# Stick-breaking attention: both heads of a narrow key block in one step, and the rounding on VectorE

## The chip, the cores and the metric

The kernel runs on one core of a Trainium2 chip. Its time is device time in microseconds (us) of one launch. The engines of the core work side by side, each through its own list of instructions in order, and wait for each other by semaphores: TensorE (PE in the rows; matrix products, results go to PSUM, eight banks of 512 fp32 columns), VectorE (DVE), ScalarE (ACT), GpSimd (POOL) and SyncE (SP, which here issues the loads).

## The reference

The kernel computes two transformer blocks over 512 tokens of width 1024. The change touches the attention of the very last layer, "stick-breaking" attention with 12 heads of 64:

```
z = einsum("bhtd,bhsd->bhts", qb, kb) * scale
causal = s_idx < t_idx
log_not = where(causal, log_sigmoid(-z), 0.0)
tail = cumsum(log_not, axis=3, reverse=True) - log_not
log_a = log_sigmoid(z) + tail
a = where(causal, exp(log_a), 0.0)
out = einsum("bhts,bhsd->bhtd", a, vb)
```

A query t gives key s the weight exp(z - sum of softplus(z) over the keys from s up to t), so each key's weight needs the sum over all later keys. All is computed to fp32 accuracy.

## The kernel before

The program is one long pipeline: feed-forward parts and projections (most of the time, TensorE's split products of lines 947 to 949), attention parts between. Weights come as units of 128 x 1024; ScalarE rounds a unit to its high part and GpSimd subtracts to get the low part. Each engine's order is written out by hand in its own function.

In the stick-breaking stage keys lie on the partitions and queries in the columns. A chunk c is a pair of heads (2c, 2c+1), which lie in the two 64-row halves of a tile; there are 6 chunks. A chunk takes its four key blocks of 128 from the last, j = 3, to the first, j = 0. Key block j is seen by 512 - 128 j queries, so the widths are 128, 256, 384, 512. A step is one head and one block (48 steps), a round is the two steps of a block (24 rounds). Step t uses PSUM bank t % 6, so three rounds are in flight. Its way is:

- TensorE `sb_scores` (L1362): z of the step.
- VectorE `sb_clip_` (L1807): min(z, 40) into a slot. ScalarE `sb_exp_ln` (L905, L907): ln(1 + exp). VectorE `sb_soft` (L1817): the maximum of that and z, which is softplus; then L1818 multiplies the 128 columns of the diagonal block by the causal mask.
- ScalarE `sb_round` (L915): the high part XH. GpSimd `low_softplus` (L481): the low part XL. Eight slots of each are kept, since the sums of a block need the later blocks of the same head.
- TensorE `sb_tail` (L1374): subtracts the sums, a product for the high and one for the low part of each block at or behind j, 2 to 8 a step, into the scores' bank. Then L1376 adds a large negative number above the diagonal.
- ScalarE `sb_weights` (L922): exp, the weights. TensorE `sb_values` (L1387): their product with v into bank 6 or 7. VectorE `sb_take` (L1800): the chunk's result out of PSUM.

What sets the order: TensorE's loop over rounds does scores of round i, tail sums of i-2 (`LAG_T` 4 steps), values of i-3 (`LAG_V` 6 steps), and scores wait until the weights of round i-3 have been taken from their bank. ScalarE does for each t: weights of step t-4, exp and ln of t, rounding of t-1. VectorE: clip of t, then maximum and mask of t-1.

Of the kernel before, what the change touches and what calls it, by code (L numbers as in the profile page):

```python
# [230 lines left out]
LAG_T = 4  # L231
LAG_V = 6
SBANKS = 6


def program(nc, xT, memT, wstream, small, consts, constsb, out):
# [4 lines left out]
    with ctx:  # L241
# [38 lines left out]
        RSTDM = sb("RSTDM", [P, M])  # L280
        PS = ctx.enter_context(nc.psum_tensor("PS", [P, 8, S], F))
# [7 lines left out]
        ASLOT = [PB[:, 2, :], PB[:, 3, :], W[:, 20, :], W[:, 21, :]]  # L289
        ESLOT = [PT[:, 0, :], PT[:, 1, :], TMP[:, 0, :], TMP[:, 1, :]]  # L290
# [83 lines left out]
        sb_l, sb_hi, sb_lo = sem("sb_l"), sem("sb_hi"), sem("sb_lo")  # L374
        sb_tri, sb_a, sb_pv, sb_o = sem("sb_tri"), sem("sb_a"), sem("sb_pv"), sem("sb_o")
# [3 lines left out]
        SBSTEPS = [(2 * c + r, j) for c in range(6) for j in range(NT - 1, -1, -1) for r in range(2)]  # L379
# [61 lines left out]
        def _(pool):  # L441
# [34 lines left out]
            def low_softplus():  # L476

                for t, (h, j) in enumerate(SBSTEPS):
                    w = S - j * P
                    pool.wait_ge(sb_hi, t + 1)  # L480
                    pool.tensor_tensor(XL[:, t % 8, 0:w], PB[:, t % 2, 0:w], XH[:, t % 8, 0:w].bitcast(F),  # L481
                                       ALU.subtract).then_inc(sb_lo, 1)
# [19 lines left out]
        def _(act):  # L502
# [398 lines left out]
            def sb_exp_ln(t):  # L901

                e = ESLOT[t % 4][:, 0:S - SBSTEPS[t][1] * P]
# [5 lines left out]
            def sb_round(t):  # L909

                w = S - SBSTEPS[t][1] * P
                act.wait_ge(sb_l, t + 1)
                if t >= 8:
                    act.wait_ge(sb_tri, t - 1)
                act.activation(XH[:, t % 8, 0:w], PB[:, t % 2, 0:w], ACT.Copy).then_inc(sb_hi, 1)  # L915

            def sb_weights(t):
                w = S - SBSTEPS[t][1] * P
# [3 lines left out]
                act.activation(ASLOT[t % 4][:, 0:w], PS[:, t % SBANKS, 0:w], ACT.Exp).then_inc(sb_a, 1)  # L922
# [21 lines left out]
        def _(pe):  # L944
# [409 lines left out]

            n = len(SBSTEPS)

            def sb_scores(t):
                h, j = SBSTEPS[t]
                if t >= SBANKS:
                    pe.wait_ge(sb_a, (t | 1) - SBANKS + 1)  # L1360
# [603 lines left out]
```

## Time and profile before

| what | us |
|---|---|
| median of three runs | 2361.65 |
| the runs | 2356.34 to 2362.01 |
| the profiled execution | 2363.2 |
| its span | 2361.4 |

TensorE is busy for 2258.7 us of the span, GpSimd 975.1, VectorE 976.8, ScalarE 841.4. The page cuts the span into 40 slices of 59 us; the stage described lies in slices 32 and 33, where TensorE's busy digits are 7 and 8, and the load engines stand nearly still (19 and 1 GB/s). "Busy" of TensorE overlaps between products that run one behind the other, so the starts of its instructions say more than their durations.

### The profile page before, as it was taken

The page shows a single profiled execution, that of the slowest core. Times are in us where ns is not written, and L with a number is a line of the kernel's source. Part 1 is how long each engine was busy: PE and PEld are TensorE (multiplying, and loading weights), DVE is VectorE, ACT ScalarE, POOL GpSimd, SP SyncE. Part 2 cuts the span into 40 slices and gives each one's busy share as a digit, 9 for nine tenths or more (in the row PEclk, how much of TensorE's full clock was granted, in tenths as well). Part 3 has the DMA queues.
Part 4 walks back from the last instruction along what each step waited for, and adds up shares of the span by engine and source line. Part 5 has one row for each costly group of instructions (what it writes and reads, how often), then busy time and mean ns, then how long its engine had stood idle before and what let it go on. Part 6 is the DMA issues. An engine that isn't in the chain of part 4 may idle for free.

```text
span 2361.4 us, 28298 instructions
## 1 busy us (share of the span) xinstructions
PE 2258.7 (96%) x10366; PEld 1781.8 (75%) x10366; DVE 976.8 (41%) x1433; ACT 841.4 (36%) x1410; POOL 975.1 (41%) x435
## 2 busy tenths in 40 slices
PE   8999999998889899999999999999999789999997
PEld 6888887874446688888777888888877458888886
DVE  3112347356674511134675421124552663211344
ACT  4222235323663422223443332222342763322222
POOL 4444444551002544444453354444443433544442
PEclk9999999998889999999999999999999989999999
DMA  5222332331001132223232232222222002322222
GB/s 184 89 106 89 107 107 89 125 125 36 1 1 38 70 107 89 107 89 118 78 107 72 90 107 91 104 89 107 80 95 76 19 1 72 122 92 93 103 89 71
DMA packets 29801, 202.67 MB, mean 86 GB/s; under 512 B 3360, under 2 KB 4000, under 8 KB 6048
## 3 DMA queue, kind: packets, MB, share of 16 engines
q1 hardware_dynamic: 28800, 198.55, 23.9%
q10 hardware_dynamic: 928, 3.14, 0.4%
q8 instruction: 46, 0.75, 0.1%
q14 instruction: 27, 0.22, 0.0%
HBM read 198.54 MB, written 2.10 MB: 85 GB/s over the span
## 4 chain that ended last, share of the span: by engine, by line
PE 87%; DVE 5%; ACT 4%; issue 2%; POOL 1%; ACTq 0%; DVEq 0%; POOLq 0%
PE PS L947 26%; PE PS L949 26%; PE PS L948 26%; PE PS L1270 1%; PE PS L1239 1%; DVE ACC L1430 1%; PE PS L1374 1%; PE PS L1198 1%; PE PS L1362 1%; DVE TMP L1510 1%; DVE NMAX L1662 1%; POOL X L471 1%; PE PS L1018 1%; PE PS L1094 0%; DVE PB L1681 0%
## 5 line engine op out<-in xcount | busy, mean ns | idle before, releaser
L446 POOL TENSOR_TENSOR WL<-RAW,WH 128x1024 fp32r<-128x1024 f32 x368 | 908.8, 2473 | 1276.0 <-ACT WH L512 1276.0
L947 PE MATMUL PS<-XH,WH 128*128 128x512 f32 (+1 forms) x2200 | 866.9, 394 | 30.4 <-DVE XL L1422 20.9
L949 PE MATMUL PS<-XH,WL 128*128 128x512 f32 (+1 forms) x2200 | 853.4, 388 | 0.0
L948 PE MATMUL PS<-XL,WH 128*128 128x512 f32 (+1 forms) x2200 | 853.1, 388 | 0.0
L512 ACT ACTIVATE WH<-RAW 128x1024 fp32r<-128x1024 f32 x368 | 388.1, 1059 | 1262.2 <-PE PS L949 1218.3
L947 PEld LDWEIGHTS PS<-XH,WH 128*128 128x128 f32 x2200 | 415.3, 189 | 126.6 <-issue 27.5
L948 PEld LDWEIGHTS PS<-XL,WH 128*128 128x128 f32 x2200 | 415.7, 189 | 85.8 <-issue 4.1
L949 PEld LDWEIGHTS PS<-XH,WL 128*128 128x128 f32 x2200 | 415.1, 189 | 84.8
L949 PE MATMUL PS<-HH,WL 128*128 128x512 f32 x672 | 261.7, 389 | 0.0
L948 PE MATMUL PS<-HL,WH 128*128 128x512 f32 x672 | 261.7, 389 | 0.0
L947 PE MATMUL PS<-HH,WH 128*128 128x512 f32 x672 | 261.7, 389 | 0.0
L1453 DVE TENSOR_TENSOR Y<-RSTD,PS 128x512 f32<-128x512 f32 x88 | 60.5, 687 | 379.9 <-PE PS L949 379.9
L1477 DVE TENSOR_TENSOR HL<-WORK,HH 128x512 fp32r<-128x512 f32 x60 | 140.8, 2346 | 185.1 <-ACT HH L671 172.8
L1451 DVE TENSOR_TENSOR TMP<-RSTD,PS 128x512 f32<-128x512 f32 x88 | 60.5, 688 | 306.0 <-PE PS L949 294.9
L949 PEld LDWEIGHTS PS<-HH,WL 128*128 128x128 f32 x672 | 126.2, 188 | 26.2
L948 PEld LDWEIGHTS PS<-HL,WH 128*128 128x128 f32 x672 | 126.2, 188 | 26.1
L947 PEld LDWEIGHTS PS<-HH,WH 128*128 128x128 f32 x672 | 126.2, 188 | 26.1
L1422 DVE SCALAR_TENSOR_TENSOR XL<-X,SM,XH 128x512 fp32r<-128x512 f32 x64 | 66.0, 1048 | 67.4 <-ACT XH L525 67.4
L1430 DVE TENSOR_TENSOR ACC<-ACC,SQ 128x512 f32<-128x512 f32 x66 | 57.2, 866 | 34.5 <-ACT SQ L534 30.3
L1456 DVE TENSOR_TENSOR WORK<-SQ,Y 128x512 f32 (+1 forms) x88 | 63.7, 723 | 18.5 <-ACT SQ L646 7.5
L1662 DVE TENSOR_REDUCE NMAX<-PS 128x1 f32<-128x256 f32 (+4 forms) x160 | 59.0, 410 | 22.9 <-PE PS L1210 12.7
L481 POOL TENSOR_TENSOR XL<-PB,XH 128x128 fp32r<-128x128 f32 (+3 forms) x48 | 41.8, 871 | 61.4 <-ACT XH L915 61.4
(194 smaller groups left out, 1639.3 us busy)
## 6 DMA issues: line engine op xcount, KB each, us to landing
RAW<-wstream SPq DMA_DIRECT2D x183, 1024.0 KB, 4.8
X<-xT SPq DMA_DIRECT2D x4, 512.0 KB, 9.4
WORK<-memT ACTq DMA_DIRECT2D x2, 1024.0 KB, 5.5
outT<-WORK SPq DMA_DIRECT2D x8, 256.0 KB, 2.1
RAW<-wstream SPq DMA_DIRECT2D x2, 512.0 KB, 6.5
PB<-WORK ACTq DMA_DIRECT2D x8, 127.8 KB, 2.4
CST<-consts SPq DMA_DIRECT2D x1, 912.0 KB, 12.1
WORK<-constsb SPq DMA_DIRECT2D x1, 256.0 KB, 12.7
```

The source lines that it names most:

```text
L446: pool.tensor_tensor(WL[:, s, :, :].rearrange("p a b -> p (a b)"), RAW[:, s, :], WH[:, s, :, :].rearrange("p a b -> p (a b)").bitcast(F), ...
L512: act.activation(WH[:, v % RING, :, :].rearrange("p a b -> p (a b)"), RAW[:, v % RING, :], ACT.Copy).then_inc(hi_done, 1)
L947: pe.matmul(o, wh, xh, start=start, stop=False)
L948: pe.matmul(o, wh, xl, start=False, stop=False)
L949: return pe.matmul(o, wl, xh, start=False, stop=stop)
L1422: dve.scalar_tensor_tensor(lo, src, gain(name, k), hi.bitcast(F), ALU.mult, ALU.subtract).then_inc(xn_ready, 1)
L1430: dve.tensor_tensor(ACC[:, :], SQ[:, 0, :] if k == 1 else ACC[:, :], SQ[:, k % 2, :], ALU.add).then_inc(sq_added, 1)
L1451: dve.tensor_tensor(TMP[:, s, :], RSTD[:, :], PS[:, 2 * s, :], ALU.mult).then_inc(g_scaled, 1)
L1453: dve.tensor_tensor(Y0[:, :], RSTD[:, :], PS[:, 2 * s + 1, :], ALU.mult).then_inc(gu_free, 1)
L1456: dve.tensor_tensor(h, SQ[:, s, :], Y0[:, :], ALU.mult).then_inc(h_ready, 1)
L1477: dve.tensor_tensor(HL[:, s, :], W[:, bass.ds(i * 2 + (s + 2), 1), :].rearrange("p a b -> p (a b)"), HH[:, s, :].bitcast(F), ALU.subtract) ...
L1662: dve.tensor_reduce(NMAX[:, s:s + 1], PS[:, score_bank(y, j), 0:y["n"]], AX.X, ALU.max, negate=True).then_inc(nmax_ready, 1)
```

## The change

Steps change. Where both heads' queries fit in a bank together (2 x width <= 512, so j = 3 and j = 2) one step holds both heads, in neighbouring columns of one bank; the blocks j = 1 and j = 0 keep a step and a bank for each head. A chunk has then six steps of widths 256, 512, 384, 384, 512, 512 and still four rounds (lists `SBSTEPS` and `SBROUNDS`). Each round has its own banks (0, 1, 2+3, 4+5), so four rounds are in flight.

The mask moves: the large negative number is added right behind the scores, before the clip, and the multiply is gone. A masked softplus is then 0 by itself. In a paired step TensorE computes the first head, adds its mask, waits for its own first product (`sb_first`) and computes the second head.

The rounding moves from ScalarE to VectorE: `sb_round` takes the same maximum a second time, straight into XH. The fp32 softplus goes to four slots (two of them in the new tile LT).

```
@@ -228,9 +228,9 @@
-LAG_T = 4
-LAG_V = 6
-SBANKS = 6
+LAG_T = 3
+LAG_V = 4
+LAG_A = 3
...
+        LSLOT = [PB[:, 0, :], PB[:, 1, :], LT[:, 0, :], LT[:, 1, :]]
...
-        SBSTEPS = [(2 * c + r, j) for c in range(6) for j in range(NT - 1, -1, -1) for r in range(2)]
+        SBSTEPS, SBROUNDS = [], []
+        for _c in range(6):
+            for _j in range(NT - 1, -1, -1):
+                _own = [(0, 1)] if 2 * (S - _j * P) <= S else [(0,), (1,)]
+                SBROUNDS.append([len(SBSTEPS) + n for n in range(len(_own))])
+                SBSTEPS += [dict(c=_c, j=_j, heads=heads, w=S - _j * P) for heads in _own]
+        SBCHUNK = len(SBSTEPS) // 6
...
+        def sb_bank(t):
+            x = SBSTEPS[t]
+            return PS[:, NT - 1 - x["j"] if len(x["heads"]) == 2 else 4 - 2 * x["j"] + x["heads"][0], 0:sb_width(t)]
...
ScalarE
-            def sb_round(t):
-                w = S - SBSTEPS[t][1] * P
-                act.wait_ge(sb_l, t + 1)
-                if t >= 8:
-                    act.wait_ge(sb_tri, t - 1)
-                act.activation(XH[:, t % 8, 0:w], PB[:, t % 2, 0:w], ACT.Copy).then_inc(sb_hi, 1)
...
-            for t in range(n + LAG_T):
-                if t >= LAG_T:
-                    sb_weights(t - LAG_T)
+            for t in range(n + LAG_A):
                 if t < n:
                     sb_exp_ln(t)
-                if 1 <= t <= n:
-                    sb_round(t - 1)
+                if t >= LAG_A:
+                    sb_weights(t - LAG_A)
...
TensorE
+            def sb_scores(i):
+                if i >= NT:
+                    pe.wait_ge(sb_a, SBROUNDS[i - NT][-1] + 1)
+                parts = [(t, h) for t in SBROUNDS[i] for h in SBSTEPS[t]["heads"]]
+                if len(SBROUNDS[i]) == 1:
+                    (t, a), (_, b) = parts
+                    sb_products(t, a).then_inc(sb_first, 1)
+                    sb_strict(t, a)
+                    pe.wait_ge(sb_first, sum(len(r) == 1 for r in SBROUNDS[:i + 1]))
+                    sb_products(t, b)
+                    sb_strict(t, b).then_inc(sb_qk, 1)
+                else:
+                    for t, h in parts:
+                        sb_products(t, h)
+                    for t, h in parts:
+                        sb_strict(t, h).then_inc(sb_qk, 1)
...
+            for i in range(len(SBROUNDS) + LAG_V):
+                if i < len(SBROUNDS):
+                    sb_scores(i)
+                if 0 <= i - LAG_T < len(SBROUNDS):
+                    for t in SBROUNDS[i - LAG_T]:
+                        sb_tail(t)
+                if i >= LAG_V:
+                    sb_values(i - LAG_V)
...
VectorE
+                dve.tensor_tensor(LSLOT[t % 4][:, 0:w], ESLOT[t % 4][:, 0:w], sb_bank(t), ALU.max).then_inc(sb_l, 1)
+            def sb_round(t):
+                w = sb_width(t)
+                dve.wait_ge(sb_ln, t + 1)
+                if sb_slot_free(t):
+                    dve.wait_ge(sb_tri, sb_slot_free(t))
+                dve.tensor_tensor(XH[:, t % 8, 0:w], ESLOT[t % 4][:, 0:w], sb_bank(t), ALU.max).then_inc(sb_hi, 1)
+            for t in range(n + SBCHUNK + 1):
                 if t < n:
                     sb_clip_(t)
+                if 2 <= t <= n + 1:
+                    sb_round(t - 2)
                 if 1 <= t <= n:
                     sb_soft(t - 1)
```

`sb_slot_free(t)` is the number of tail sums after which the high part's slot of step t is free. In the new kernel's rows below L1378 is the score product, L1382 the mask addition, L1413 the tail sums, L1426 the values; on VectorE L1845 the clip, L1853 the maximum, L1861 the rounding maximum; on ScalarE L936 and L938 exp and ln, L944 the weights.

TensorE before, from the tail sums of a 256-wide round to the scores of the next chunk's 128-wide round (x2: both heads):

```order
L1374 MATMUL PS<-XH,SUMS 128x256
L1374 MATMUL PS<-XL,SUMS 128x256
L1374 MATMUL PS<-XH,SUMS 128x128
L1374 MATMUL PS<-XL,SUMS 128x128
L1376 MATMUL PS<-CSB 128x128
L1374 MATMUL PS<-XH,SUMS 128x256
L1374 MATMUL PS<-XL,SUMS 128x256
L1374 MATMUL PS<-XH,SUMS 128x128
L1374 MATMUL PS<-XL,SUMS 128x128
L1376 MATMUL PS<-CSB 128x128
L1387 MATMUL PS<-PB,WORK 64x128 x2
L1362 MATMUL PS<-WORK 128x128 x2
```

TensorE after, the same kind of place:

```order
L1426 MATMUL PS<-PB,WORK 64x512 x2
L1378 MATMUL PS<-WORK 128x128
L1382 MATMUL PS<-CSB 128x128
L1378 MATMUL PS<-WORK 128x128
L1382 MATMUL PS<-CSB 128x128
L1413 MATMUL PS<-XH,SUMS 128x256
L1413 MATMUL PS<-XL,SUMS 128x256
L1413 MATMUL PS<-XH,SUMS 128x128
L1413 MATMUL PS<-XL,SUMS 128x128
L1413 MATMUL PS<-XH,SUMS 128x256
L1413 MATMUL PS<-XL,SUMS 128x256
L1413 MATMUL PS<-XH,SUMS 128x128
```

The two narrow score products no longer stand next to each other; each has its mask addition behind it, and the mask additions are gone from the tail sums.

ScalarE before, from an exp of a 512-wide step (TMP and PT are the slots, PB and WORK take weights):

```order
L905 ACTIVATE TMP<-TMP 128x512
L907 ACTIVATE TMP<-TMP 128x512
L915 ACTIVATE XH<-PB 128x384
L922 ACTIVATE WORK<-PS 128x256
L905 ACTIVATE TMP<-TMP 128x512
L907 ACTIVATE TMP<-TMP 128x512
L915 ACTIVATE XH<-PB 128x512
L922 ACTIVATE PB<-PS 128x384
```

ScalarE after, from the weights of a 512-wide step:

```order
L944 ACTIVATE PB<-PS 128x512
L936 ACTIVATE PT<-PT 128x384
L938 ACTIVATE PT<-PT 128x384
L944 ACTIVATE PB<-PS 128x512
L936 ACTIVATE PT<-PT 128x384
L938 ACTIVATE PT<-PT 128x384
L944 ACTIVATE WORK<-PS 128x256
```

The rounding into XH has left the list, and between two weights there are only exp and ln.

VectorE before, around 128-wide and 256-wide steps:

```order
L1807 TENSOR_SCALAR PT<-PS 128x128
L1817 TENSOR_TENSOR PB<-PT,PS 128x128
L1818 TENSOR_TENSOR PB<-PB,CST 128x128
L1807 TENSOR_SCALAR TMP<-PS 128x256
L1817 TENSOR_TENSOR PB<-PT,PS 128x128
L1818 TENSOR_TENSOR PB<-PB,CST 128x128
L1807 TENSOR_SCALAR TMP<-PS 128x256
L1817 TENSOR_TENSOR PB<-TMP,PS 128x256
L1818 TENSOR_TENSOR PB<-PB,CST 128x128
```

VectorE after, around 384-wide and 512-wide steps:

```order
L1845 TENSOR_SCALAR PT<-PS 128x384
L1861 TENSOR_TENSOR XH<-TMP,PS 128x512
L1853 TENSOR_TENSOR PB<-PT,PS 128x384
L1845 TENSOR_SCALAR TMP<-PS 128x512
L1861 TENSOR_TENSOR XH<-PT,PS 128x384
L1853 TENSOR_TENSOR PB<-PT,PS 128x384
L1845 TENSOR_SCALAR TMP<-PS 128x512
L1861 TENSOR_TENSOR XH<-PT,PS 128x384
L1853 TENSOR_TENSOR LT<-TMP,PS 128x512
```

The short multiply (L1818) has gone; a second full-width maximum, into XH, stands before the next step's maximum.

## Rows read from the trace of the kernel before

**Rows 1.** The page's first line, and the busy shares under it.

```profile
span 2361.4 us, 28298 instructions
...
PE 2258.7 (96%) x10366; PEld 1781.8 (75%) x10366; DVE 976.8 (41%) x1433; ACT 841.4 (36%) x1410; POOL 975.1 (41%) x435
```

**Rows 2.** Windows, the stage: length, busy time by engine, clock, DMA share, GB/s.

```profile
1833.00:1942.00 109.00, 86.00 (x484) 56.06 (x484) 71.61 (x150) 78.59 (x198) 43.70 (x49) 0.89 0.01 2
```

**Rows 3.** Waits, 1833 to 1942: us in total, times, longest.

```profile
ACT XH L915 <- PE PS L1376: 21.6, 19, 2.3
...
PEld PS L1362 <- ACT PB L922: 17.0, 11, 1.7
...
PEld PS L1362 <- ACT WORK L922: 14.3, 10, 2.1
```

**Rows 4.** Timeline of TensorE, one chunk: start, duration, instruction, idle before it.

```profile
1867.47 0.70 PE L1362 MATMUL PS<-WORK 64*128 64x256 f32 x4 [1.13 <-ACT PB L922]
...
1868.10 0.50 PE L1374 MATMUL PS<-XH,SUMS 128*128 128x512 f32 x1
...
1870.94 0.87 PE L1387 MATMUL PS<-PB,WORK 128*64 128x384 f32 x4
...
1872.14 0.92 PE L1362 MATMUL PS<-WORK 64*128 64x384 f32 x4 [0.33 <-ACT WORK L922]
...
1873.73 1.08 PE L1387 MATMUL PS<-WORK 128*64 128x512 f32 x4
...
1875.67 1.13 PE L1362 MATMUL PS<-WORK 64*128 64x512 f32 x4 [0.86 <-ACT PB L922]
...
1876.73 0.39 PE L1374 MATMUL PS<-XH,SUMS 128*128 128x256 f32 x1
...
1877.93 0.44 PE L1387 MATMUL PS<-PB,WORK 128*64 128x128 f32 x4
...
1880.28 0.49 PE L1362 MATMUL PS<-WORK 64*128 64x128 f32 x4 [1.91 <-ACT WORK L922]
...
1880.70 0.45 PE L1374 MATMUL PS<-XH,SUMS 128*128 128x384 f32 x1
...
1882.63 0.65 PE L1387 MATMUL PS<-WORK 128*64 128x256 f32 x4
...
1884.41 0.70 PE L1362 MATMUL PS<-WORK 64*128 64x256 f32 x4 [1.13 <-ACT PB L922]
```

**Rows 5.** The chain of waits, start and end of the stage: start, us, what.

```profile
1834.47 0.51 PE PS L1362 x4
...
1850.64 0.70 PE PS L1362 x4
...
1941.66 0.69 DVE WORK L1800
```

**Rows 6.** Groups by shape, 1828 to 1945: busy us, mean ns, idle before.

```profile
L1818 DVE TENSOR_TENSOR PB<-PB,CST 128x128 f32<-128x128 f32 x48 | 26.3, 547 | 1.6
...
L1817 DVE TENSOR_TENSOR PB<-TMP,PS 128x512 f32<-128x512 f32 x12 | 8.3, 688 | 1.6 <-ACT TMP L907 1.0
...
L907 ACT ACTIVATE TMP<-TMP 128x512 f32<-128x512 f32 x12 | 7.6, 632 | 0.4
...
L915 ACT ACTIVATE XH<-PB 128x512 fp32r<-128x512 f32 x12 | 7.5, 625 | 4.9 <-PE PS L1376 3.1 <-DVE PB L1818 1.7
...
L922 ACT ACTIVATE WORK<-PS 128x512 f32<-128x512 f32 x12 | 7.0, 584 | 2.1 <-PE PS L1376 2.1
...
L915 ACT ACTIVATE XH<-PB 128x128 fp32r<-128x128 f32 x12 | 3.6, 302 | 9.9 <-PE PS L1376 9.8
...
L1807 DVE TENSOR_SCALAR PT<-PS 128x128 f32<-128x128 f32 x12 | 3.3, 282 | 2.9 <-PE PS L1362 2.9
```

**Rows 7.** Timeline of all engines: a GpSimd subtraction and a VectorE multiply.

```profile
1848.12 1.28 POOL L481 TENSOR_TENSOR XL<-PB,XH 128x512 fp32r<-128x512 f32 x1 [0.97 <-ACT XH L915]
...
1848.28 1.27 DVE L1818 TENSOR_TENSOR PB<-PB,CST 128x128 f32<-128x128 f32 x1
```

More of the change, by code:

```diff
@@ L1353, in _, with sb_products @@
             pe.wait_ge(turned, FLIPS[max(FLIPS)]["c"])
[L1355 to L1360, printed above, removed]
-                r = slice(DH * (h % 2), DH * (h % 2) + DH)
-                pe.matmul(PS[:, t % SBANKS, 0:S - j * P], W[r, 8 + h // 2, j * P:(j + 1) * P],
-                          Q[r, h // 2, j * P:S], start=True, stop=True).then_inc(sb_qk, 1)
+            def sb_products(t, h):
+                x = SBSTEPS[t]
+                c, j, r = x["c"], x["j"], slice(DH * h, DH * h + DH)
+                return pe.matmul(sb_bank(t)[:, sb_cols(t, h)], W[r, 8 + c, j * P:(j + 1) * P], Q[r, c, j * P:S],
+                                 start=h == x["heads"][0], stop=False, skip_group_check=True)
@@ L1365, in sb_tail @@
             def sb_tail(t):
-                h, j = SBSTEPS[t]
-                w = S - j * P
+                x = SBSTEPS[t]
+                c, j, w = x["c"], x["j"], x["w"]
                 pe.wait_ge(sb_lo, t + 1)
-                bank = PS[:, t % SBANKS, :]
-                for n in range(NT - j):
-                    col, width, m = n * P, w - n * P, SUMS[:, 1 if n == 0 else 0, :]
-                    for part in (XH, XL):
-                        pe.matmul(bank[:, col:w], m, part[:, (t - 2 * n) % 8, 0:width], start=False,
-                                  stop=False, skip_group_check=True)
@@ L1390, in _ @@
-            pe.wait_ge(sums_ready, 1)
-            for t in range(0, n + LAG_V, 2):
-                if t < n:
-                    sb_scores(t)
-                    sb_scores(t + 1)
-                if 0 <= t - LAG_T < n:
-                    sb_tail(t - LAG_T)
-                    sb_tail(t + 1 - LAG_T)
-                if t >= LAG_V:
-                    pe.wait_ge(sb_a, t - LAG_V + 2)
-                    sb_values(t - LAG_V)
-                    sb_values(t + 1 - LAG_V)
+                for h in x["heads"]:
+                    bank = sb_bank(t)[:, sb_cols(t, h)]
+                    for n in range(NT - j):
+                        src, m = sb_step(c, j + n, h), SUMS[:, 1 if n == 0 else 0, :]
+                        for part in (XH, XL):
+                            mm = pe.matmul(bank[:, n * P:w], m, part[:, src % 8, sb_cols(src, h)], start=False,
+                                           stop=n == NT - j - 1 and part is XL, skip_group_check=True)
@@ new lines, in sb_tail, with sb_values @@
+                mm.then_inc(sb_tri, 1)
+            def sb_values(i):
+                pe.wait_ge(sb_a, SBROUNDS[i][-1] + 1)
+                for t in SBROUNDS[i]:
+                    x = SBSTEPS[t]
+                    c, j = x["c"], x["j"]
+                    if j == NT - 1 and c >= 2:
+                        pe.wait_ge(sb_o, c - 1)
+                    for h in x["heads"]:
+                        mm = pe.matmul(PS[DH * h:DH * h + DH, 6 + c % 2, j * P:S],
+                                       V_SB[:, j, c * P + h * DH:c * P + (h + 1) * DH],
+                                       ASLOT[t % 4][:, sb_cols(t, h)],
+                                       start=j == NT - 1, stop=j == 0, skip_group_check=True)
+                    mm.then_inc(sb_pv, 1)
```

62 lines of the change are left out of this document (29 added, 33 removed).

## The prediction

> **What bounds the kernel now.** I read the page's busy shares first [rows 1]: TensorE is busy nearly all the time, so only places where it waits are worth anything. The change touches one stage, stick-breaking attention of the last layer, which the chain of waits puts between 1834.47 us (first score product) and 1941.66 us (the last copy out of PSUM) [rows 5]: 107.2 us, 4.5% of the span. No engine is full there: over the stretch 1833 to 1942 TensorE has 86.0 us of work in 109, ScalarE 78.6, VectorE 71.6, GpSimd 43.7 [rows 2]. The table of waits says who holds whom [rows 3]: TensorE's next score products wait for ScalarE's attention weights (L922), 17.0 + 14.3 us as its weight loads see it, and ScalarE's rounding (L915) stands idle for 21.6 us in front of a TensorE result. It is a ring: products, softplus, tail sums, weights, and the products that need the freed bank.
>
> TensorE's own timeline over one chunk (two heads, four key blocks, so four rounds) gives the period [rows 4]. The 256-wide scores start at 1867.47 and again at 1884.41: 16.94 us a chunk. The idle times on the four score rows that end in it are 0.33, 0.86, 1.91 and 1.13: 4.23 us. So TensorE's work is 16.94 - 4.23 = 12.71 us a chunk. That number and those four gaps carry the forecast.
>
> The same rows show that a pair of heads costs little more than one. From the 256-wide scores to the tail sum behind them are 0.63 us (1867.47 to 1868.10), from the 512-wide ones 1.06 (1875.67 to 1876.73): 1.68 ns a column for both heads and 0.20 us fixed. The two heads stream side by side, since they use different 64 rows of the array.
>
> **The change part by part.**
>
> ScalarE loses its rounding pass. L915 runs from 0.302 us (128 wide) to 0.625 (512) [rows 6]; in a straight line 0.41 and 0.52 between, so 2 x 1.85 = 3.7 us a chunk. With six wider steps instead of eight, exp, ln and weights also lose six fixed parts. ScalarE goes from 78.6 / 6 = 13.1 us a chunk to about 9. More than the sum, it is the order that counts: behind one weights pass there is now exp and ln only before the next one, no wait for VectorE's maximum and no rounding.
>
> VectorE loses the mask multiply (L1818, 8 a chunk x 0.547 = 4.4 us) and gains a second maximum that writes XH. By 0.282 us for the clip at 128 and 0.688 for the maximum at 512 [rows 6], clip and maximum alike, one pass over widths 256, 512, 384, 384, 512, 512 costs 0.42 + 3 x 0.69 + 2 x 0.55 = 3.6 us; three passes and one 0.68 copy are 11.4 us a chunk, before 3.9 + 3.9 + 4.4 + 0.7 = 12.9 (71.6 / 6 = 11.9 as measured, since neighbours overlap a little). That a rounding maximum with one operand in PSUM costs 0.688 like L1817 is read from that row; from above I bound it by the 1.27 us of a VectorE instruction held up by GpSimd [rows 7], which would make 6 x 0.6 = 3.5 us more a chunk, 14.9 in all and still below the period; from below nothing is gained over L1817. I take 0.688, because L1817 has the same operands. The 128-wide mask multiply took 1.27 us beside a GpSimd instruction of 1.28 that began 0.16 us earlier [rows 7]; its two inputs are in SBUF. The Trainium skill (SBUF — State Buffer, Who interferes with whom) says that a VectorE instruction with two SBUF inputs contends with GpSimd reads and one with at most one does not; the trace agrees as far as L1818 goes, and by that rule the change removes the only contended instruction.
>
> GpSimd's subtraction keeps its length (1.28 us at 512 [rows 7]), about 43.7 / 6 = 7 us a chunk; with four buffers for its input VectorE no longer waits for it. I cost this at nothing beyond the ring below. DMA and SP aren't touched.
>
> TensorE keeps all products. The eight mask additions (bf16, 128 wide) move from the end of the tail sums to the scores: the same number, 0 us net. What is new is the narrow rounds: their two heads now write one bank, so they run one behind the other, with a wait of TensorE for its own first product between. Lower bound: just the streaming that was side by side, 128 x 1.67 ns = 0.21 and 256 x 1.67 = 0.43, so 0.64 us a chunk. Upper bound by these rows: the 0.20 us fixed part four more times (each of the two rounds goes once more to the mask addition and once more back), 1.44 us. I take 1.1, in the middle, since the first mask addition covers part of the wait. Behind the waiting instruction stands all of TensorE's queue, so the 1.1 us count in full. The Trainium skill (TensorEngine Tiling (Array Packing), Key Properties) says that changing the tiling mode drains TensorE; narrow rounds now change three times where they changed once. By that rule the 1.44 would hold, and the saving below would be some 2 us smaller. No row separates a drain from a load here.
>
> The waits that stay. The round loop is the same ring with one round more in flight: in iteration i come scores of round i, tail sums of i-3, values of i-4, and scores i+1 need the weights of the tail sums just done. So the last tail product is followed by about 0.4 us until ScalarE starts (its own 0.3 us and 0.1 for the signal, an estimate), by ScalarE's pass, and by 0.05 us; of that the values products (0.44 to 1.08 us: the 128-wide ones of 1877.93 and 512-wide ones of 1873.73 [rows 4]) cover a part. Widths between are taken 0.84 ns a column below the 512 rows of [rows 6] (the slope of L915): exp and ln 0.42 each at 256 and 0.52 at 384, weights 0.48 at 384. The tail sums of one head are half of the 2.84 us from 1868.10 to 1870.94 (512) or of the 1.93 from 1880.70 to 1882.63 (384), less 0.1 for the mask addition that leaves. Round by round, for the tail sums of the
>
> - 256-wide pair: one step for both heads, so nothing can start early, 0.4 + 0.58 (L922) + 0.05 against 0.1 + 0.44 of cover: 0.5 us wait;
> - 384-wide: weights, exp and ln of a 256-wide step, weights again, 0.4 + 0.48 + 0.84 + 0.48 + 0.05 = 2.25 from the first head's end against 0.87 + 0.1 + 0.65 of cover: 0.6;
> - 512-wide: the same with 0.4 + 0.58 + 1.04 + 0.58 + 0.05 = 2.65 against 1.3 + 0.1 + 0.87: 0.35;
> - 128-wide pair: covered by the 1.08 us of values, 0.
>
> Together 1.4 us in place of 4.23. The new period is 12.71 + 1.1 + 1.4 = 15.2 us. Nothing else comes late in it: VectorE's rounding of a step stands behind the clip two steps later, but tail sums come three rounds (over 10 us) after the scores, and the path there (clip 0.69, exp and ln 1.26, two maxima 1.4, GpSimd 1.27) is 4.6 us.
>
> Both ends. Before, the first five rounds took 1850.64 - 1834.47 = 16.2 us [rows 5], waiting for one latency after the other. Now four rounds of scores go ahead at once; following the first steps in the same way I get to scores 5 after about 11 us, and allow 12.5 because TensorE may well be at its low clock there. What is left of the 107.2 us before is 91.0: four chunks (67.8) and 23.2 for the last three rounds and the draining. After: 4 x 15.2 = 60.8, and about 22.5, since one more round drains. Sum 12.5 + 60.8 + 22.5 = 95.8 us, against 107.2: **11.4 us saved**.
>
> The profiled execution took 2363.2 us, 1.8 outside its span of 2361.4 [rows 1], and 1.55 over the median 2361.65 of the three runs. The difference is applied to the median: **2350.2 us**. Runs here spread over 5.7 us, so I count less than 0.3% (7.1 us) as no change.
>
> **The clock.** Over the stage the granted clock averages 0.89 [rows 2], so TensorE spends about a fifth of it at the 1.2 GHz level, with a gap of 1.91 us in every chunk as the longest [rows 4]. With these gaps smaller I expect no more low time than before, and count no gain.
>
> **Rivals.**
> 1. The wait moves and hardly shrinks. ScalarE's queue is in order: each wide round still has exp and ln between its two weights, and VectorE's loop now puts three passes into each step. If TensorE's waits come to 2.6 us instead of 1.4, and start-up gains 2 us, the period is 12.71 + 1.1 + 2.6 = 16.4, so 5 x 0.5 + 2 = 4.5 us saved: 2357.2 us, no change to measure. For it: all four engines have over half of the period to do. Against: ScalarE has 10 us in 15.
> 2. Slower: the serial narrow rounds. If a wait of TensorE for itself, with the two extra turns, costs 2.5 us a narrow round, the period is 12.71 + 5.0 + 1.4 = 19.1, over 5.5 chunks 12 us longer, less 3.7 at the start: +8 us, 2370 us. It decides from 1.7 us a narrow round on (2 x 1.7 = 4.23 - 1.4 + 3.7 / 6). Against: changes between scores, tails and values in [rows 4] cost tenths of a microsecond.
> 3. More than forecast: no wait is left and the clock stays up. Period 12.71 + 0.8 = 13.5, start-up 11: 5 x 3.4 + 2 = 19 us, 2343 us. For it: with 13.8 us of work TensorE would be nearly full. Against: one-step weights in the narrow rounds can't start early.
>
> **Chances.** Forecast 0.62 (its own range 2345 to 2356), rival 1 0.19, rival 2 0.08, rival 3 0.11. Faster by over 0.3%: nearly all of the forecast (0.59) and rival 3, 0.70. Slower: rival 2 and a rest, 0.09. Same: 0.21. The range for 8 in 10 takes rival 1 in and most of rival 3: 2342 to 2359.
>
> **What would show it.** In the profile after: no ScalarE copy into XH and no multiply on VectorE in the stage; VectorE's two maxima at 0.69 us each at 512; TensorE idle in front of scores near 1.4 us a chunk; the second narrow product starting 0.4 to 0.8 us after the first; a period near 15.2 us; five rounds by about 12 us. It would be wrong if TensorE idles over 3 us a chunk, if the period is TensorE's work alone but that has grown by over 2 us, if VectorE's maxima stretch beside GpSimd, or if most of the stage runs at the low clock.

## The result, and the profile after

The changed kernel took 2348.92 us in the median of six runs (2344.57 to 2350.45), the kernel before 2360.43 in six (2356.34 to 2362.01): a ratio of 0.9945, with an interval from 0.9934 to 0.9957. That is 11.5 us between the medians (0.55%), clear of the noise; the prediction had 11.4.

The page's first line and busy shares after, which answer to [rows 1]:

```profile
span 2346.7 us, 28096 instructions
...
PE 2261.3 (96%) x10366; PEld 1782.0 (76%) x10366; DVE 966.5 (41%) x1397; ACT 820.1 (35%) x1326; POOL 973.1 (41%) x423
```

The window of the stage itself, from the first score product to the last copy, as in [rows 2] (length, TensorE, its weight loads, VectorE, ScalarE, GpSimd, clock, DMA share, GB/s). Before, the same stretch was 107.19 us long (1834.47 to 1941.66, [rows 5]):

```profile
1836.19:1927.57 91.38, 86.73 (x480) 54.37 (x480) 60.66 (x113) 55.70 (x111) 39.87 (x37) 0.94 0.00 1
```

TensorE does the same 480 products and now has work nearly all the time (86.73 us in 91.38); over the same stretch of each kernel ScalarE's work fell from 77.2 to 55.7 us and VectorE's from 71.3 to 60.7. The stage is 15.8 us shorter in these two profiles; the part ahead of the stage happened to be 1.7 us longer, the part behind it 0.6 shorter, which no edit explains (over all profiles here the stage's start lies between 1829.1 and 1836.2). So I read effects below from the stage and the period of a chunk, and use the whole time as the check.

The waits, 1833 to 1930, in the columns of [rows 3]:

```profile
ACT WORK L944 <- PE PS L1413: 18.4, 14, 3.2
...
ACT PB L944 <- PE PS L1413: 12.5, 10, 1.5
...
PEld PS L1378 <- ACT PB L944: 7.9, 11, 0.9
...
PEld PS L1378 <- ACT WORK L944: 6.2, 9, 0.8
```

TensorE's waits for weights ahead of the scores fell from 17.0 + 14.3 to 7.9 + 6.2 us. ScalarE still waits for tail sums, but now with its weights pass itself, no longer with a rounding that then stands in front of that pass.

TensorE's timeline over one chunk, the rows that answer to [rows 4] (start, duration, instruction, idle before):

```profile
1863.59 0.70 PE L1378 MATMUL PS<-WORK 64*128 64x256 f32 x2 [0.32 <-ACT WORK L944]
1864.22 0.23 PE L1382 MATMUL PS<-CSB 128*128 128x128 bf16 x1
1864.38 0.70 PE L1378 MATMUL PS<-WORK 64*128 64x256 f32 x2
1865.01 0.23 PE L1382 MATMUL PS<-CSB 128*128 128x128 bf16 x1
1865.05 0.42 PE L1413 MATMUL PS<-XH,SUMS 128*128 128x384 f32 x1
...
1867.77 0.92 PE L1378 MATMUL PS<-WORK 64*128 64x384 f32 x4 [0.32 <-ACT PB L944]
...
1871.38 0.87 PE L1426 MATMUL PS<-PB,WORK 128*64 128x384 f32 x4
1872.32 1.13 PE L1378 MATMUL PS<-WORK 64*128 64x512 f32 x4
...
1875.05 0.48 PE L1378 MATMUL PS<-WORK 64*128 64x128 f32 x2
1875.47 0.23 PE L1382 MATMUL PS<-CSB 128*128 128x128 bf16 x1
1875.63 0.48 PE L1378 MATMUL PS<-WORK 64*128 64x128 f32 x2
1876.05 0.23 PE L1382 MATMUL PS<-CSB 128*128 128x128 bf16 x1
1876.09 0.36 PE L1413 MATMUL PS<-XH,SUMS 128*128 128x256 f32 x1
...
1877.89 0.70 PE L1378 MATMUL PS<-WORK 64*128 64x256 f32 x2 [0.32 <-ACT PB L944]
```

The period is 1877.89 - 1863.59 = 14.30 us (16.94 before). The idle times on the score rows are 0.32 + 0.32 = 0.64 us (4.23 before), so the work is 13.66 us against 12.71: 0.95 more. The stretches of the rows say where it arises. From the first score product to the first tail sum the narrow rounds take 1.46 us (256) and 1.04 (128), before 0.63 and 0.42, which is 1.45 more with their mask additions in it. The wide rounds take 0.19 more by their mask additions, and the four stretches of tail sums are together 0.68 shorter without them (the 384-wide one 1.74 us from 1865.05 to 1866.79, before 1.93). Between first and second product of a narrow round are 0.79 us (256) and 0.58 us (128).

### The profile page after: what moved, and what is told of

Same layout as the page of the kernel before. It is cut to its first block, busy times and chain, and to the rows that moved or that the text cites. A ratio compares the mean times of both kernels' runs of the same rounds, so it can differ in the third digit from the quotient of the medians.

```text
span 2346.7 us, 28096 instructions
## 1 busy us (share of the span) xinstructions
PE 2261.3 (96%) x10366; PEld 1782.0 (76%) x10366; DVE 966.5 (41%) x1397; ACT 820.1 (35%) x1326; POOL 973.1 (41%) x423
## 4 chain that ended last, share of the span: by engine, by line
PE 89%; DVE 5%; ACT 3%; issue 2%; POOL 1%; DVEq 0%; ACTq 0%; POOLq 0%
PE PS L967 27%; PE PS L969 27%; PE PS L968 27%; PE PS L1259 1%; PE PS L1290 1%; PE PS L1378 1%; PE PS L1218 1%; PE PS L1413 1%; DVE ACC L1469 1%; DVE NMAX L1701 1%; DVE TMP L1549 1%; PE PS L1038 1%; POOL X L502 1%; PE PS L1114 0%; POOL WL L477 0%
## 5 line engine op out<-in xcount | busy, mean ns | idle before, releaser
L1492 DVE TENSOR_TENSOR Y<-RSTD,PS 128x512 f32<-128x512 f32 x88 | 60.5, 687 | 379.9 <-PE PS L969 379.9
L1490 DVE TENSOR_TENSOR TMP<-RSTD,PS 128x512 f32<-128x512 f32 x88 | 60.5, 688 | 306.0 <-PE PS L969 294.9
L1469 DVE TENSOR_TENSOR ACC<-ACC,SQ 128x512 f32<-128x512 f32 x66 | 57.2, 866 | 34.5 <-ACT SQ L565 30.3
L1495 DVE TENSOR_TENSOR WORK<-SQ,Y 128x512 f32 (+1 forms) x88 | 63.7, 723 | 18.5 <-ACT SQ L677 7.4
L556 ACT ACTIVATE XH<-X,SM 128x512 fp32r<-128x512 f32 x56 | 39.5, 720 | 56.2 <-POOL X L502 32.1
```

The source lines that it names most:

```text
L1469: dve.tensor_tensor(ACC[:, :], SQ[:, 0, :] if k == 1 else ACC[:, :], SQ[:, k % 2, :], ALU.add).then_inc(sq_added, 1)
L1490: dve.tensor_tensor(TMP[:, s, :], RSTD[:, :], PS[:, 2 * s, :], ALU.mult).then_inc(g_scaled, 1)
L1492: dve.tensor_tensor(Y0[:, :], RSTD[:, :], PS[:, 2 * s + 1, :], ALU.mult).then_inc(gu_free, 1)
L1495: dve.tensor_tensor(h, SQ[:, s, :], Y0[:, :], ALU.mult).then_inc(h_ready, 1)
```

## The experiments

All ratios are to the kernel before on the same chip. "Stage" runs from the first score product to the last copy out of PSUM, "period" from one 256-wide score product to the next at full clock, both from the profiled execution.

| kernel | ratio (interval) | stage, us | period, us |
|---|---|---|---|
| before | 1 | 107.2 | 16.94 |
| changed | 0.9945 (0.9934 to 0.9957) | 91.4 | 14.30 |
| e1, slot wait narrowed | 0.997 (0.996 to 0.998) | 102.9 | 16.23 |
| e2, mask early | 0.9998 (0.9989 to 1.0007) | 108.3 | 16.85 |
| e3, no pairs, three rounds | 0.9929 (0.9913 to 0.9945) | 92.9 | 14.57 |
| e4, ScalarE rounds | 0.9955 (0.9938 to 0.9971) | 99.4 | 15.34 |
| e5, pairs, three rounds | 1.0061 (1.0049 to 1.0074) | 128.9 | 18.2 and up |
| e6, wide rounds serial | 0.9989 (0.9979 to 0.9999) | 109.3 | 16.41 |
| e7, one turn | 0.9932 (0.9916 to 0.9949) | 94.7 | 14.34 |
| e8, weights together | 0.992 (0.9906 to 0.9934) | 92.4 | 13.83 |
| e9, e5 with earlier rounding | 0.9969 (0.9958 to 0.998) | 102.1 | 15.56 |
| e10, e3 with weights together | 0.992 (0.9905 to 0.9934) | 89.7 | 14.06 |
| e11, e8 again | 0.9934 (0.992 to 0.9948) | 90.8 | 13.83 |
| e12, changed again | 0.9942 (0.9928 to 0.9957) | 94.4 | 14.30 |

The stage of one and the same kernel differs by some 3 us between profiles (91.4 and 94.4, granted clock 0.94 and 0.91), the period by 0.02; so the period is the sharper number.

### Which part carries the gain

**e1**, the kernel before with one wait narrowed:

```
                 if t >= 8:
-                    act.wait_ge(sb_tri, t - 1)
+                    act.wait_ge(sb_tri, t - 7 + 2 * SBSTEPS[t - 8][1])
```

> The kernel before with one wait narrowed: ScalarE's rounding of step t waits only until the last reader of its slot is done (t - 7 + 2j tail sums, j the block of step t - 8) instead of for the tail sums of step t - 2 always. Theory A (the gain of the change comes from what ScalarE no longer does between a tail sum and the weights): the 21.6 us in which L915 stood idle for a tail sum mostly go, the rounding gets out of the way of the weights, and each round's wait of TensorE shrinks by 0.3 us or more: 4 to 9 us faster than before. Theory B (four rounds in flight and paired steps are what helps): under 2 us. Theory C (all of the gain was this too strict wait): 10 us or more.

Measured: 4.9 us between the medians, 4.3 in the stage, 0.71 in the period. ScalarE's L915 still waited for tail sums, but 9.9 us in place of 21.6:

```profile
ACT XH L915 <- PE PS L1376: 9.9, 5, 2.4
```

So theory A at its lower end, though nearly half of the 21.6 us stayed. The edit was part of the change (`sb_slot_free` also asks for less), and the prediction did not price it apart: the old rule made the rounding of a step wait for the tail sums of the step before last, though its slot had long been read. For the 128-wide steps the edit changes nothing (j = 3 gives t - 1 again), and all of the wait that is left stands there, 9.8 us before and 9.9 in this run:

```profile
L915 ACT ACTIVATE XH<-PB 128x128 fp32r<-128x128 f32 x12 | 3.6, 302 | 10.0 <-PE PS L1376 9.9
```

Of TensorE's four waits a chunk only two shrank as theory A had it (0.86 to 0.50 us ahead of the 512-wide scores, 1.91 to 1.43 ahead of the 128-wide ones); 0.33 stayed and 1.13 became 1.26. In the changed kernel a chunk has six steps, fewer than there are slots, so there the 128-wide step waits only for the chunk before last.

**e2**, the mask ahead of the clip in the kernel before:

```
+                    sb_strict(t)
+                    sb_strict(t + 1)
...
-                chain(dve.tensor_tensor(lt[:, 0:w], ESLOT[t % 4][:, 0:w], PS[:, t % SBANKS, 0:w], ALU.max))
-                dve.tensor_tensor(lt[:, 0:P], lt[:, 0:P], CST[:, K_MASK:K_MASK + P], ALU.mult).then_inc(sb_l, 1)
+                dve.tensor_tensor(lt[:, 0:w], ESLOT[t % 4][:, 0:w], PS[:, t % SBANKS, 0:w], ALU.max).then_inc(sb_l, 1)
```

> The kernel before with the mask added right behind the two heads' scores, ahead of the clip, and no multiply on VectorE; all else stays. Theory A: VectorE's 26 us of multiplies were beside the path (ScalarE waited 1.7 us for them in all), so 0 to 3 us faster. Rival (the multiply that GpSimd holds up to 1.27 us was on the ring): 5 us or more faster. In both the clips start about 0.2 us later a round.

Measured: no change. VectorE's work in the stage fell from 71.3 to 45.9 us, and the time did not move: that was idle capacity, though multiplies beside GpSimd ran up to 1.35 us in the kernel before (1.27 in [rows 7]). TensorE's four waits are 0.32, 0.94, 1.98 and 1.20 us here, 4.44 in all, so its work is 16.85 - 4.44 = 12.41 us a chunk: moving the mask additions takes 0.30 us off TensorE's work, and the waits grew by 0.21. That the early mask makes room on VectorE for the second maximum is argued from VectorE's sum; no run has the second maximum without it.

**e3**, mask early, rounding on VectorE, four softplus slots and the narrowed slot wait, but the old steps, banks and three rounds:

```
+            def sb_round(t):
+                w = S - SBSTEPS[t][1] * P
+                dve.wait_ge(sb_ln, t + 1)
+                if t >= 8:
+                    dve.wait_ge(sb_tri, t - 7 + 2 * SBSTEPS[t - 8][1])
+                dve.tensor_tensor(XH[:, t % 8, 0:w], ESLOT[t % 4][:, 0:w], PS[:, t % SBANKS, 0:w], ALU.max).then_inc(sb_hi, 1)
...
+                if 2 <= t <= n + 1:
+                    sb_round(t - 2)
```

> The kernel before with early mask, rounding on VectorE as a second maximum, four softplus slots and the narrowed slot wait, but its eight steps a chunk, its six banks and three rounds in flight: all heads' scores side by side. Theory A: as fast as the changed kernel or up to 3 us faster (no serial narrow rounds, 0.95 us a chunk, but the start is slower), 10 to 15 us under before, period 13.7 to 14.5 us. Theory B (depth and pairing carry the gain): less than half of it, 5 us or less under before, period above 15.5 us.

Measured: 16.7 us between the medians, as much as the changed kernel gains or more, without a paired step and without a fourth round. Its period lies 0.07 us above my band. TensorE's score rows in it, and one row of the tail sums:

```profile
1856.33 0.70 PE L1354 MATMUL PS<-WORK 64*128 64x256 f32 x4
...
1860.52 0.92 PE L1354 MATMUL PS<-WORK 64*128 64x384 f32 x4
...
1863.53 1.13 PE L1354 MATMUL PS<-WORK 64*128 64x512 f32 x4 [0.41 <-ACT PB L916]
...
1867.27 0.49 PE L1354 MATMUL PS<-WORK 64*128 64x128 f32 x4 [1.09 <-ACT WORK L916]
...
1869.27 0.45 PE L1370 MATMUL PS<-XH,SUMS 128*128 128x384 f32 x1 [0.48 <-POOL XL L483]
...
1870.90 0.70 PE L1354 MATMUL PS<-WORK 64*128 64x256 f32 x4
```

Here TensorE idles 0.41 + 1.09 us ahead of scores and 0.48 ahead of the second head's 384-wide tail sums, for GpSimd's low part: 1.98 us a chunk, in the changed kernel 0.64. But its work is only 14.57 - 1.98 = 12.59 us, against 13.66 with serial narrow rounds. The two nearly cancel: 14.57 against 14.30.

**e4**, the changed kernel with the rounding on ScalarE:

```
                 if t < n:
                     sb_exp_ln(t)
+                if 1 <= t <= n:
+                    sb_round(t - 1)
                 if t >= LAG_A:
```

> The changed kernel with the rounding back on ScalarE as a copy between ln and the weights; paired steps, four rounds in flight and early mask stay. Theory A: the copy of 0.4 to 0.6 us stands again before some of the weights, TensorE's waits grow by 0.3 to 0.5 us in three of four rounds: 4 to 8 us slower than the changed kernel, 4 to 8 us faster than before. Theory B: with a round more in flight ScalarE has time, within 2 us of the changed kernel.

Measured: period 15.34, 1.04 more than the changed kernel, and a stage of 99.4 against 91.4 and 94.4. The whole time, by its ratio, lies only 0.001 above the changed kernel's, with intervals that overlap (about 2.4 us, under the 4 of theory A): by that alone it could not be told. The period gives theory A, 1.04 us a chunk. The idle times say where the microsecond is (0.32 both in the changed kernel and none ahead of the 512-wide scores):

```profile
1869.95 0.92 PE L1387 MATMUL PS<-WORK 64*128 64x384 f32 x4 [0.84 <-ACT PB L951]
...
1875.02 1.13 PE L1387 MATMUL PS<-WORK 64*128 64x512 f32 x4 [0.59 <-ACT WORK L951]
...
1880.59 0.70 PE L1387 MATMUL PS<-WORK 64*128 64x256 f32 x2 [0.32 <-ACT PB L951]
```

The waits grow by 0.52 and 0.59 us in the two wide rounds, where ScalarE has work between two weights, and not at all in the narrow ones. The comparison also reads the other way: with the rounding on ScalarE the changed kernel still keeps 1.60 of its 2.64 us a chunk (15.34 against 16.94), of which the slot wait and the mask, measured from the kernel before, are 0.8.

### Depth and the order of the rounding

**e5**, the changed kernel with three rounds in flight:

```
-LAG_T = 3
-LAG_V = 4
-LAG_A = 3
+LAG_T = 2
+LAG_V = 3
+LAG_A = 2
+DEPTH = 3
...
-                if i >= NT:
-                    pe.wait_ge(sb_a, SBROUNDS[i - NT][-1] + 1)
+                if i >= DEPTH:
+                    pe.wait_ge(sb_a, SBROUNDS[i - DEPTH][-1] + 1)
```

> The changed kernel with three rounds in flight instead of four: scores of round i wait for the weights of round i - 3, tail sums follow two rounds behind, values three, weights two steps behind exp and ln. Banks, paired steps and rounding on VectorE stay. Theory A (the length of the way from a tail sum to the weights sets the wait, and the 4.6 us from scores to low parts fit into two rounds as well): 0 to 3 us slower than the changed kernel. Theory B (depth carries the gain): 8 us or more slower, with TensorE waiting for GpSimd's low parts.

Measured: the largest miss of the study. I had said 0 to 3 us; it is slower than the kernel before. Its timeline shows the chain (all engines, TensorE's weight loads left out):

```profile
1899.53 0.56 DVE L1846 TENSOR_SCALAR PT<-PS 128x384 f32<-128x384 f32 x1 [4.41 <-PE PS L1383]
1900.01 0.41 DVE L1862 TENSOR_TENSOR XH<-TMP,PS 128x256 fp32r<-128x256 f32 x1
...
1900.50 0.73 POOL L513 TENSOR_TENSOR XL<-LT,XH 128x256 fp32r<-128x256 f32 x1 [4.36 <-DVE XH L1862]
...
1901.28 0.33 PE L1414 MATMUL PS<-XH,SUMS 128*128 128x128 f32 x1 [1.73 <-POOL XL L513]
```

VectorE sits for 4.41 us in a clip whose scores TensorE has not issued; behind it waits the rounding of a step that was ready, behind that GpSimd, and behind that TensorE. The rounding stands behind the clip two steps on. In e3 two steps are one round; with paired steps they are two rounds.

**e9** takes that order away and keeps three rounds:

```
-                if 2 <= t <= n + 1:
-                    sb_round(t - 2)
                 if 1 <= t <= n:
                     sb_soft(t - 1)
+                    sb_round(t - 1)
```

> The run with three rounds in flight, with VectorE's order altered: maximum and rounding maximum of step t - 1 right behind the clip of step t, instead of the rounding of step t - 2. Theory A' (three rounds were slow because the rounding stands behind the clip two steps on, and with paired steps that is a clip whose scores TensorE issues in the very round whose tail sums need the rounding): the waits of TensorE for GpSimd's low parts (15.3 and 13.4 us) mostly go and the stage falls from 128.9 to 92 to 100 us. Theory B (paired steps need four rounds whatever the order): the stage stays above 110 us.

Measured: 26.8 us of the stage come back (128.9 to 102.1), 2 us short of my band; TensorE's waits for GpSimd's low parts fell from 21.8 and 18.5 us over the whole stage (its weight loads, its products; the 15.3 and 13.4 above are the part up to 1930 us) to 2.8 and 1.9. So the order was most of the damage. The rest, 15.56 against 14.30 in the period, is wait for ScalarE's weights: 0.29 + 0.52 + 0.32 + 0.75 = 1.88 us ahead of scores for 0.64 in the changed kernel. It is what three rounds cost with paired steps in this order; e9 differs from the changed kernel in VectorE's order too, so depth alone is not measured.

### The price of serial rounds

**e6** makes the wide rounds serial as well:

```
-                    for t, h in parts:
-                        sb_products(t, h)
-                    for t, h in parts:
-                        sb_strict(t, h).then_inc(sb_qk, 1)
+                    (t, a), (u, b) = parts
+                    sb_products(t, a).then_inc(sb_first, 1)
+                    sb_strict(t, a).then_inc(sb_qk, 1)
+                    pe.wait_ge(sb_first, i + 1)
+                    sb_products(u, b)
+                    sb_strict(u, b).then_inc(sb_qk, 1)
```

> The changed kernel with the two wide rounds of a chunk made serial as well: product, mask addition, wait for the own product, second product, mask addition. It measures the price of a serial round by itself. The narrow rounds give 0.58 and 0.79 us from the first product to the second, of which the mask addition was there before. If that is just lost side by side streaming and two more turns, the wide ones cost 384 x 1.67 ns = 0.64 and 0.85 us, plus 0.16 us each: 1.8 us a chunk, 11 us over the stage. If part of it only fills waits for ScalarE that are there anyway, 7 to 10 us slower than the changed kernel. If the wait of TensorE for itself is nearly free and products overlap, under 4 us.

Measured: 2.11 us a chunk more (1.8 expected), 109.3 in the stage against 91.4 and 94.4, so nearly all of the gain is gone (ratio 0.9989). The second product starts 1.00 us after the first at 384 columns:

```profile
1873.42 0.91 PE L1378 MATMUL PS<-WORK 64*128 64x384 f32 x2 [0.31 <-ACT PB L944]
...
1874.42 0.91 PE L1378 MATMUL PS<-WORK 64*128 64x384 f32 x2
```

It is 1.22 us at 512. My 1.8 counted the columns and the 0.16, and left out the 0.20 us fixed part of each product. Serial rounds count in full: the waits of 0.32 us ahead of the 256-wide and 384-wide scores stayed as they were. Six chunks' worth is 12.7 us. What the stage grew beyond that lies mostly in its first five rounds, which took 17.93 us at a mean granted clock of 0.52, against 10.97 at 0.78 and 12.80 at 0.66 in the two profiles of the changed kernel.

**e7** leaves the wait and takes two of the three turns between 64-row and 128-row products away:

```
-                    sb_strict(t, a)
                     pe.wait_ge(sb_first, sum(len(r) == 1 for r in SBROUNDS[:i + 1]))
                     sb_products(t, b)
+                    sb_strict(t, a)
                     sb_strict(t, b).then_inc(sb_qk, 1)
```

> The changed kernel with both products of a narrow round one behind the other (the wait between them stays) and both mask additions behind them: one turn from products to mask additions instead of three. If the turns between 64-row and 128-row products cost much, the second product starts earlier than 0.58 and 0.79 us after the first, and the kernel gains 1 us or more. If the wait for the first product sets the second's start, it stays at about 0.55 and 0.75 us, the masks cost about 0.1 us behind it, and the time stays within 1 us of the changed kernel's.

Measured: nothing gained (period 14.34). From the first 256-wide product to the tail sums are 1865.03 - 1863.55 = 1.48 us, in the changed kernel 1865.05 - 1863.59 = 1.46:

```profile
1863.55 1.45 PE L1378 MATMUL PS<-WORK 64*128 64x256 f32 x4 [0.32 <-ACT WORK L944]
1864.93 0.29 PE L1382 MATMUL PS<-CSB 128*128 128x128 bf16 x2
1865.03 0.42 PE L1413 MATMUL PS<-XH,SUMS 128*128 128x384 f32 x1
```

The row of the two products is merged, so the second one's own start isn't seen. If that product takes its 0.63 us to the mask addition as elsewhere, it starts at about 1864.30, 0.75 us after the first (an estimate), and the two mask additions take 0.10 behind it. Two turns fewer gain nothing; what costs is that the second product runs behind the first.

### A better order on ScalarE

**e8** and **e11** are one kernel: in wide rounds ScalarE takes both heads' weights one behind the other, without exp and ln between.

```
-            for t in range(n + LAG_A):
+            for t in range(n + LAG_A + 1):
                 if t < n:
                     sb_exp_ln(t)
-                if t >= LAG_A:
-                    sb_weights(t - LAG_A)
+                last = t - LAG_A
+                if 0 <= last < n and SBSTEPS[last]["j"] >= 2:
+                    sb_weights(last)
+                elif 0 <= last < n and SBSTEPS[last]["heads"] == (0,):
+                    sb_weights(last)
+                    sb_weights(last + 1)
```

> The changed kernel with ScalarE's order altered in the wide rounds: the weights of both heads come one behind the other instead of with an exp and ln between. Theory A: the wait of TensorE ahead of 384-wide scores (0.32 us) falls to about 0.1 or 0.2, so the period goes from 14.3 to about 14.1 us and the kernel gains 0 to 2 us. Rival: exp and ln come later by a weights pass, the softplus path gets late, and the kernel loses 1 us or more.

> The changed kernel with both heads' weights one behind the other, once more, beside the changed kernel itself: 1 to 4 us faster than that, period 13.8 us as before.

ScalarE's timeline, first the changed kernel, then e8, from the first weights of the 384-wide round:

```profile
1866.09 0.49 ACT L944 ACTIVATE PB<-PS 128x384 f32<-128x384 f32 x1 [1.37 <-PE PS L1413]
1866.48 0.41 ACT L936 ACTIVATE PT<-PT 128x256 f32<-128x256 f32 x1
1866.92 0.42 ACT L938 ACTIVATE PT<-PT 128x256 f32<-128x256 f32 x1
1867.24 0.47 ACT L944 ACTIVATE PB<-PS 128x384 f32<-128x384 f32 x1
```

```profile
1865.47 0.49 ACT L944 ACTIVATE PB<-PS 128x384 f32<-128x384 f32 x1 [1.37 <-PE PS L1417]
1866.28 0.49 ACT L944 ACTIVATE PB<-PS 128x384 f32<-128x384 f32 x1 [0.32 <-PE PS L1417]
```

The second weights begin 0.81 us after the first instead of 1.15; the wait ahead of the 384-wide scores is gone, the period 13.83 us. That is 0.47 us less, more than the 0.1 to 0.2 I expected. The row of the 384-wide scores gives 0.32 of it. The other 0.15 lie ahead of the 512-wide scores, whose row showed no idle time though they did wait: they started 0.94 us after the 384-wide values (1871.38 to 1872.32), here 0.80, and the chain of the changed kernel has the weights right ahead of them:

```profile
1871.68 0.59 ACT WORK L944
...
1872.32 1.13 PE PS L1378 x4
```

A busy time that is modelled can hide a short wait; the starts of neighbouring instructions show it. The medians were 2345.71 us (e8) and, beside the changed kernel itself (e12, 2348.17), 2344.85 us (e11): 3.3 us less than that, more than the 0 to 2 expected for e8, with intervals of the ratios that overlap slightly (0.992 to 0.9948 and 0.9928 to 0.9957).

> The changed kernel unaltered, for comparison on the same chip: 10 to 14 us under the kernel before, period 14.3 us.

**e10** does the same to e3:

```
-            for t in range(n + LAG_T):
+            for t in range(0, n + LAG_T, 2):
                 if t >= LAG_T:
                     sb_weights(t - LAG_T)
+                    sb_weights(t - LAG_T + 1)
                 if t < n:
                     sb_exp_ln(t)
+                    sb_exp_ln(t + 1)
```

> The run without paired steps (eight steps a chunk, three rounds in flight, rounding on VectorE, early mask), with ScalarE's order altered: the weights of both heads of a round one behind the other, then exp and ln of both. TensorE's waits there are 1.09 us ahead of 128-wide scores and 0.41 ahead of 512-wide ones. If the exp and ln between the two weights make them: they fall by half or more, the period goes from 14.6 to 13.4 to 14.0 us and the stage from 92.9 to 86 to 90 us. If three rounds leave too little time for exp and ln to come later: period 14.5 us or more.

Measured: 2341.66 us median, the lowest of all (the changed kernel in the same comparison 2348.17, e11 2344.85; e8's ratio of 0.992 is the same), stage 89.7. The period of 14.06 just misses my band: its score rows show no idle time any longer at full clock, but the wait of TensorE's tail sums for GpSimd's low parts, 4.0 us in e3, has grown. It is 12 waits, in most chunks two ahead of the 384-wide tail sums (0.16 and 1.10 us):

```profile
PE PS L1372 <- POOL XL L483: 7.8, 12, 1.1
```

What makes it late can be read from the other engines' rows of one such place:

```profile
1878.13 0.52 ACT L909 ACTIVATE PT<-PT 128x384 f32<-128x384 f32 x1
...
1880.73 0.68 DVE L1806 TENSOR_SCALAR TMP<-PS 128x512 f32<-128x512 f32 x1
...
1881.33 0.54 DVE L1823 TENSOR_TENSOR XH<-PT,PS 128x384 fp32r<-128x384 f32 x1
...
1883.00 0.44 PE L1372 MATMUL PS<-XH,SUMS 128*128 128x384 f32 x1 [1.10 <-POOL XL L483]
```

The ln of that step ended at 1878.65, and its rounding began 2.7 us later, behind five passes that VectorE ran one after the other from 1878.59 on, the last the clip of two steps on. So exp and ln were not late. The first reading was right about the waits for weights; what holds the kernel now is VectorE's queue, the same order as in e5. No run here changes that order in e10. Its period is longer than e8's and its stage about as long, and it needs neither pairs nor a fourth round.

## Why the prediction was right

- **The period**: 15.2 us predicted, 14.30 measured. The waits were 0.64 for a predicted 1.4, and TensorE's work grew by 0.95 for a predicted 1.1. That 0.95 is two terms. The prediction set the moved mask additions at 0; e2 shows that they take 0.30 off. Against e2's work of 12.41 the serial narrow rounds then cost 1.25 a chunk, inside the bounds of 0.64 and 1.44 and 0.15 over the value taken.
- **The waits** were in the right places with too large sizes: 0.5, 0.6, 0.35 and 0 predicted, 0.32, 0.32, 0 and 0 on the rows (0.15 for the third by e8). Two terms were too long. The 0.4 us from a last tail product to ScalarE's start was 0.31 (a product begun at 1876.93, the weights at 1877.24 by the chain). And the prediction added ScalarE's passes end to end, where each starts before the one ahead of it has ended: from the first 384-wide weights to the second, with exp and ln between, it took 0.48 + 0.84 = 1.32 us, and the rows in the section on e8 show 1867.24 - 1866.09 = 1.15.
- **The ends**: five rounds by 12.5 us predicted, 1847.16 - 1836.19 = 10.97 measured. Four chunks took 1906.49 - 1847.16 = 59.3 us (60.8 predicted), the rest 21.1 (22.5). Sum 91.4 against 95.8. In e12, the same kernel, the three parts are 12.80, 60.5 and 21.1, the stage 94.4. The kernel before had 16.2, 69.35 and 21.7: the prediction took its four chunks at 67.8, as if all ran at full clock, and put the 1.6 us left over into the last rounds. So the stage gained 15.8 and 12.8 us in the two profiles for a predicted 11.4, and the medians 11.5 and, in the later comparison, 13.6. That the first median hits 11.4 so closely is partly luck.
- **VectorE's second maximum** at 512 columns: 0.677 and 0.678 us (0.688 taken), as against 0.684 and 0.683 for the other maximum, so neither its fp32r output nor GpSimd beside it costs anything that shows.

```profile
L1861 DVE TENSOR_TENSOR XH<-TMP,PS 128x512 fp32r<-128x512 f32 x9 | 6.1, 678 | 0.0
...
L1861 DVE TENSOR_TENSOR XH<-PT,PS 128x512 fp32r<-128x512 f32 x9 | 6.1, 677 | 0.0
```

- **ScalarE's relief** as the source of the gain: it is shown to be enough by itself, not to be the only way. From the side of the changed kernel the rounding is worth 1.04 us a chunk (e4), the slot wait from the side of before 0.71 (e1), the mask about 0.1 (e2), and all of them without pairs and depth 2.37 of 2.64 us (e3). What e1, e2 and e4 leave of the 2.37, 0.5 us, no run here takes apart; the four softplus slots are in it. Without the rounding's move, pairs, depth and the rest still gave 1.60 (e4), so the parts overlap and do not add up.
- **The clock**: "no more low time than before" held (0.89 before, 0.94 and 0.91 after). It plays no part in the period, which is read at full clock. Over the four middle chunks the low level gave nothing back: they took 69.35 us for 4 x 16.94 = 67.8 before (1.6 more), and 59.3 and 60.5 for 4 x 14.30 = 57.2 after (2.1 and 3.3 more). In the first five rounds the mean was 0.68 before and 0.78 and 0.66 after, and the same kernel took 10.97 and 12.80 us for them. So a stage's length moves by 1.8 us there with the clock.
- **Rival 2** (serial rounds dear enough to lose) had its price measured: 1.25 us a chunk in the narrow rounds, not the 3.4 from which it decides; with two more serial rounds a chunk it comes to 1.25 + 2.11 = 3.4, and e6 shows nearly all of the gain gone there. The upper bound of 1.44 was not reached, and e7 shows no cost of the turns. For the rule that the Trainium skill gives (TensorEngine Tiling (Array Packing), Key Properties: a change of tiling mode drains TensorE) this means that a drain, if there is one, does not show here: one turn took 1.48 us and three took 1.46. It may lie within the wait that the second product has anyway. **Rival 1** fell with the 0.64 us of waits, **rival 3** would have needed 13.5 us; e8 comes to 13.83.

One claim of the prediction was unsafe without having done harm: that nothing else comes late, since the way from scores to low parts is 4.6 us. That sum left out that VectorE's rounding stands behind a clip of a later round. With four rounds there is room for it; e5 shows what it does with three.

## What to carry to other kernels

In a ring of engines look first at what stands in each in-order queue right ahead of the instruction that frees the ring: moving the rounding off ScalarE, with the early mask, the narrower slot wait and two slots more, brought the period from 16.94 to 14.57 us without pairing or a further round (14.30 with both), and putting exp and ln behind both heads' weights took either kernel about 0.5 us further (14.06 and 13.83). A lag counted in steps changes its meaning when steps are merged; recount it in rounds before reducing the depth. A wait on low parts can come from the order in a third engine's queue (e5, e10), so follow it to the first engine that had its input ready. And a wait on slots should name the last reader: the coarse one cost 5 us here and looked like a wait for data.

## What the runs showed of the hardware

Two fp32 products of 64 rows in different halves of the array run side by side so fully that one costs what two cost: 0.63 us from the 256-wide pair to the next product before [rows 4], and 1864.22 - 1863.59 = 0.63 us from a single one to its mask addition after. Putting both in one bank, with a wait between them as this program does, gives that half away. A product that waits for the one before it starts 0.58, 0.79, 1.00 and 1.22 us after it at 128, 256, 384 and 512 columns, which is the 0.42, 0.63, 0.84 and 1.06 of the product and 0.16 more, with a mask addition between; without one it is about 0.12 more, by the estimate from e7's rows.
